# Experts' weights loaded with neighbouring rows in a partition, and transposes that take every 8th and every 2nd column

## The chip, the cores and the metric

The kernel runs on one core of a Trainium2 chip. The metric is the time of the program on the device, in microseconds (us), as the median of several runs. The engines are named as in the profile: PE is TensorE's matmuls and PEld its weight loads, DVE is VectorE, ACT is ScalarE, POOL is GpSimd and SP is SyncE, which here only issues DMAs. An engine's name with a q (SPq) is its sequencer.

## What is computed

One step of a one-layer encoder for 640 tokens (512 of a new stream, 8 x 16 of running ones): projections, a short convolution, differential attention, a gated merge, a layer norm, and then a mixture of experts. Only the last part is touched. Each token goes to 2 of 32 experts:

```
def expert_step(acc, ws):
    wgu, wd, g = ws
    a, b = jnp.split(x @ wgu, 2, axis=-1)
    return acc + g[:, None] * ((jax.nn.silu(a) * b) @ wd), None
```

`wgu` is w_gate_up of one expert, 1024 x 512 in float32 (2 MB), and `wd` is w_down, 256 x 1024 (1 MB). Everything is float32. A product of two float32 matrices is made of three matmuls on parts: an operand is split into a rounded part (hi, type fp32r) and the rest (lo), and hi x hi, hi x lo and lo x hi are added up in PSUM.

## The kernel before

`project_and_attend` does the projections and attention (up to about 820 us), `route` the output product, the norm and the choice of experts, `run_experts` the experts, `combine` the weighted sum and the last norm. The order on each engine is written out by hand, with semaphores between the engines.

`run_experts` goes through 32 blocks of up to 128 token rows, one for each expert (a spare stretch for experts with more tokens isn't entered when none has more). All that a block j needs is double buffered by its parity, except the split weights of gate and up, which exist once. Its steps, by engine:

- SP (`body` in the sync block) loads w_gate_up into `up_raw` (tiles first_up and second_up, by parity) when DVE has split the one before in that buffer (wait on `up_lo_done`), then w_down into `down_raw` (first_down, second_down) when `down_lo_done` allows. A partition holds rows p, p + 128, p + 256, ... (`(k p) n -> p k n`): 8 separate rows of 2 KB of w_gate_up, 2 of 4 KB of w_down. The loads of experts 0 to 2 are issued in `route` (`load_expert`, L1004 and L1007), the others at L1353 and L1355.
- POOL gathers the block's token rows from h_rows in HBM into `rows` (L1368, an indirect DMA of up to 128 rows of 4 KB; a place without a token moves no row) and scatters finished rows to y_choice (L1375). Its order is gather j + 2, scatter j - 1, gather j + 3, scatter j, ...; a scatter waits until ACT and DVE have both copied their half of the result.
- PE (`body`): `turn_rows` of block j + 1 (8 transposes of 128 x 128, L1403, four into each of two PSUM banks), `gate_up` of j (24 matmuls with 512 columns, L1413 to L1415), `down` of j - 1 (12, L1435 to L1437), `turn_act` of j (2 transposes, L1423).
- ACT: copies the turned rows as xT_hi (L1474), splits w_down (L1469, 2 casts) and w_gate_up (L1462, 4 casts), Silu (L1491), copies the left half of the result (L1480), aT_hi (L1498).
- DVE: xT_lo (L1521, 2), the rest part of w_down (L1534, 2) and of w_gate_up (L1515, 4), act_rows (L1540), the right half of the result (L1527), aT_lo (L1546).

In a transpose the data are PE's stationary operand (they are read by the weight load) and the identity is streamed. The contraction of gate and up runs over 1024 features, 128 at a time: the transpose k gives the 128 features that must stand on the same partitions as the weights' rows of part k.

Of the kernel before, what the change touches and what calls it, by code (L numbers as in the profile page):

```python
# [32 lines left out]
P = 128  # L33
D = 1024
KT = D // P
# [893 lines left out]
def route(nc, d, keep):  # L929

    with ExitStack() as ctx:
# [5 lines left out]
        ident = const[:, C_ID:C_ID + P]  # L937

        up, down = keep["up_raw"][0], keep["down_raw"][0]
# [44 lines left out]
        @block.sync  # L984
        def _(sp):
            for k in range(2, KT):
                sp.dma_start(w_raw[k], d["w_out"][0, P * k:P * (k + 1), :]).then_inc(w_loaded[k], 16)
            for k in range(2, 4):
                sp.dma_start(x_rows[:, k - 2], d["x_prompt"][0, P * (k - 2):P * (k - 1), :]).then_inc(x_loaded[k - 2], 16)
            sp.dma_start(column[:], d["const"][:, C_COLUMN:C_END]).then_inc(small_in, 16)  # L990
            sp.dma_start(ln_g, d["ln1_g"].to_broadcast((P, D))).then_inc(small_in, 16)
            sp.dma_start(ln_b, d["ln1_b"].to_broadcast((P, D))).then_inc(small_in, 16)
            sp.dma_start(b_router[:, 0:4], d["b_group"].to_broadcast((P, 4))).then_inc(small_in, 16)
            sp.dma_start(b_router[:, 4:36], d["b_router"].to_broadcast((P, 32))).then_inc(small_in, 16)
            sp.dma_start(w_router[:, :, 0:4], d["w_group"][0].rearrange("(k p) n -> p k n", p=P)).then_inc(small_in, 16)
            sp.dma_start(w_router[:, :, 4:36], d["w_router"][0].rearrange("(k p) n -> p k n", p=P)).then_inc(small_in, 16)

            def load_expert(e, par):

                if e == 0:  # L1000
                    sp.wait_ge(split_lo, KT)
                if e > 1:
                    sp.wait_ge(keep["up_lo_done"], 4 * (e - 1))
                sp.dma_start(keep["up_raw"][par][:], d["w_gate_up"][0, e].rearrange("(k p) n -> p k n", p=P)).then_inc(keep["up_in"][par], 16)  # L1004
                if e > 1:
                    sp.wait_ge(keep["down_lo_done"], 2 * (e - 1))
                sp.dma_start(keep["down_raw"][par][:], d["w_down"][0, e].rearrange("(k p) n -> p k n", p=P)).then_inc(keep["down_in"][par], 16)  # L1007

            load_expert(0, 0)
            for b in range(2, TB):  # L1010
                src = d["x_prompt"][0, P * b:P * (b + 1), :] if b < QB else d["x_sample"].rearrange("s q d -> (s q) d")

                sp.wait_ge(taken, b - 1)
                sp.dma_start(x_rows[:, b % 2], src).then_inc(x_loaded[b % 2], 16)
            for b in range(TB):
                sp.wait_ge(h_ready, b + 1)
                sp.dma_start(d["h_rows"][P * b:P * (b + 1), :], h[:, b, :]).then_inc(h_stored[b % 2], 16)

            sp.wait_ge(out_done, TB)
            load_expert(1, 1)  # L1020

            sp.dma_start(keep["ln2_g"], d["ln2_g"].to_broadcast((P, D))).then_inc(keep["ln2_in"], 16)
            sp.dma_start(keep["ln2_b"], d["ln2_b"].to_broadcast((P, D))).then_inc(keep["ln2_in"], 16)
            load_expert(2, 0)
            sp.wait_ge(h_stored[0], 48)
            sp.wait_ge(h_stored[1], 32)
# [261 lines left out]
def run_experts(nc, d, keep):  # L1288


    with ExitStack() as ctx:
# [4 lines left out]
        ident = const[:, C_ID:C_ID + P]  # L1296

        up_raw, down_raw, (up_hi, up_lo), (down_hi, down_lo) = keep["up_raw"], keep["down_raw"], keep["up_parts"], keep["down_parts"]
        rows, y_rows = keep["rows"], keep["y_rows"]
        xT_hi, xT_lo = sb("xT_hi", [P, 2, KT, P], F32R), sb("xT_lo", [P, 2, KT, P], F32R)  # L1300
        silu, act_rows = sb("silu", [P, DE]), sb("act_rows", [P, DE])
# [3 lines left out]
        bank_x = [pb("bank_x0"), pb("bank_x1")]  # L1305
        bank_a = pb("bank_a")
# [3 lines left out]
        up_in, down_in, up_hi_done, up_lo_done, down_hi_done, down_lo_done = (  # L1310
            keep[n] for n in ("up_in", "down_in", "up_hi_done", "up_lo_done", "down_hi_done", "down_lo_done"))
# [26 lines left out]
        @block.sync  # L1338
        def _(sp):
            def body(j, n, par, first, last):  # L1340
                if not isinstance(j, int) and keep["spare"]:
                    e = sp.value_load(eid[0:1, bass.ds(j - EXPERTS, 1)], min_val=0, max_val=EXPERTS - 1)
                elif keep["spare"]:
                    e = sp.value_load(eid[0:1, j - EXPERTS:j - EXPERTS + 1], min_val=0, max_val=EXPERTS - 1)
                else:
                    e = j if isinstance(j, int) else sp.snap(j)
                up = d["w_gate_up"][0, bass.ds(e, 1)].rearrange("a (k p) n -> p (a k) n", p=P)
                down = d["w_down"][0, bass.ds(e, 1)].rearrange("a (k p) n -> p (a k) n", p=P)
                if isinstance(j, int) and j < 3:
                    return  # L1350

                wait(sp, up_lo_done, 4 * j - 4)
                sp.dma_start(up_raw[par][:], up).then_inc(up_in[par], 16)  # L1353
                wait(sp, down_lo_done, 2 * j - 2)
                sp.dma_start(down_raw[par][:], down).then_inc(down_in[par], 16)  # L1355

            def stretch(j0, j1):
                keep["spare"] = j0 > 0
                run(sp, body, j0, j1)

            all_blocks(sp, stretch)
# [32 lines left out]
        @block.tensor  # L1394
        def _(pe):
            def turn_rows(j, n, par):
                pe.wait_ge(rows_in[par], 16 * (n + 1))
                for half in range(2):

                    wait(pe, x_lo_done, 2 * j - 1 + half)  # L1400
                    for k in range(4):
                        kk = 4 * half + k
                        last = pe.transpose(bank_x[half][:, P * k:P * (k + 1)], rows[:, par, P * kk:P * (kk + 1)], ident)  # L1403
                    last.then_inc(x_turned, 1)

            def gate_up(j, par):
                pe.wait_ge(x_lo_done, 2 * j + 2)

                wait(pe, act_done, j - 1)
                for k in range(KT):  # L1410
                    if k % 2 == 0:
                        pe.wait_ge(up_lo_done, 4 * j + k // 2 + 1)
                    pe.matmul(bank_g[par][:], xT_hi[:, par, k, :], up_hi[:, k, :], start=(k == 0), stop=False)  # L1413
                    pe.matmul(bank_g[par][:], xT_hi[:, par, k, :], up_lo[:, k, :], start=False, stop=False)  # L1414
                    last = pe.matmul(bank_g[par][:], xT_lo[:, par, k, :], up_hi[:, k, :], start=False, stop=(k == KT - 1))  # L1415
                    if k % 2 == 1:
                        last.then_inc(up_used, 1)

            def turn_act(j):
                pe.wait_ge(act_done, j + 1)  # L1420
                wait(pe, a_lo_done, j)
                for k in range(2):
                    last = pe.transpose(bank_a[:, P * k:P * (k + 1)], act_rows[:, P * k:P * (k + 1)], ident)  # L1423
                last.then_inc(a_turned, 1)

            def down(j, par):
                pe.wait_ge(a_lo_done, j + 1)

                wait(pe, y_left, j)
                wait(pe, y_right, j)  # L1430
                for k in range(2):
                    pe.wait_ge(down_lo_done, 2 * j + k + 1)
                    for strip in range(2):
                        cols = slice(512 * strip, 512 * (strip + 1))
                        pe.matmul(bank_d[strip][:], aT_hi[:, k, :], down_hi[:, par, k, cols], start=(k == 0), stop=False)  # L1435
                        pe.matmul(bank_d[strip][:], aT_hi[:, k, :], down_lo[:, par, k, cols], start=False, stop=False)
                        last = pe.matmul(bank_d[strip][:], aT_lo[:, k, :], down_hi[:, par, k, cols], start=False, stop=(k == 1))  # L1437
                    last.then_inc(down_used, 1)

            def body(j, n, par, first, last):  # L1440
                if not last:
                    turn_rows(j + 1, n + 1 if par else n, 1 - par)
                gate_up(j, par)
                if not first:
                    down(j - 1, 1 - par)
                turn_act(j)

            def stretch(j0, j1):
                turn_rows(j0, j0 // 2, 0)
                run(pe, body, j0, j1)  # L1450
                down(j1 - 1, (j1 - 1) % 2)

            all_blocks(pe, stretch)
# [272 lines left out]
```

## Time and profile before

| | |
|---|---|
| median of 3 runs | 1324.09 us (1317.96 to 1324.95) |
| span of the profiled execution | 1320.7 us |
| PE busy | 1195.9 us, 91% |
| PE weight loads busy | 1062.5 us, 80% |
| DVE busy | 758.8 us, 57% |
| ACT busy | 588.1 us, 45% |
| DMA moved | 210.37 MB in 194986 packets, mean 159 GB/s |

Every row of the trace is from one execution, so sums of rows are made against its span of 1320.7 us. A share of busy time is a mean over stages with different limits; the experts' stage is about the last quarter. The time of a DMA "to landing" runs from its issue by the engine to its last byte. A packet is one contiguous piece moved by one of the 16 DMA engines; a DMA from or to 128 partitions is spread over all 16. q1 is the queue of DMAs that SP issues, q0 of those that POOL issues.

### The profile page before, as it was taken

The numbers are of one execution on the slowest core, as the hardware profiler recorded it, in microseconds if no ns is written. First come the engines' busy times: TensorE is split into PE (matmuls) and PEld (weight loads), VectorE is DVE, ScalarE is ACT, GpSimd is POOL, SyncE is SP. The second block draws the span as 40 slices with busy tenths as digits, with TensorE's granted clock in tenths as the row PEclk, the third lists the DMA queues.
The fourth block names the chain that finished last, engine by engine and source line by source line (L and its number), as shares of the span: only waits on it lengthen the run. The fifth ranks groups of instructions, "written<-read, shape, count | busy, mean of one in ns | idle before, by whom it ended". The sixth has DMA issues, their size and how long they took to land. (4 is left out here: it accounts for less than half of the span.)

```text
span 1320.7 us, 20288 instructions
## 1 busy us (share of the span) xinstructions
PE 1195.9 (91%) x7032; PEld 1062.5 (80%) x7032; DVE 758.8 (57%) x1358; ACT 588.1 (45%) x998; POOL 110.7 (8%) x96
## 2 busy tenths in 40 slices
PE   6999999999999999999989998982788999889965
PEld 5999999899998999989879897872677777677742
DVE  4325264352643526445265555448688998888936
ACT  3232333333344242442456433221677777677722
POOL 2000000000000000000000000004112122222212
PEclk9999999999999999999989998985799999999988
DMA  6522415234152331514313244625499999999814
GB/s 154 163 85 71 126 56 151 68 89 119 43 151 67 102 107 52 153 55 114 115 56 87 78 128 181 197 75 195 152 313 330 321 332 340 337 339 320 300 49 200
DMA packets 194986, 210.37 MB, mean 159 GB/s; under 512 B 14322, under 2 KB 141810, under 8 KB 194948
## 3 DMA queue, kind: packets, MB, share of 16 engines
q1 hardware_dynamic: 171680, 188.07, 44.1%
q0 software_dynamic: 9664, 11.11, 2.5%
q10 hardware_dynamic: 13604, 10.69, 2.4%
q8 instruction: 22, 0.36, 0.1%
q14 instruction: 16, 0.13, 0.0%
HBM read 200.19 MB, written 32.71 MB: 176 GB/s over the span
## 5 line engine op out<-in xcount | busy, mean ns | idle before, releaser
L318 PE MATMUL bank_u<-x_hi,w_hi 128*128 128x320 f32 (+1 forms) x1024 | 323.9, 316 | 0.4 <-ACT hist_T L512 0.4
L319 PE MATMUL bank_u<-x_lo,w_hi 128*128 128x320 f32 (+1 forms) x1024 | 319.5, 312 | 0.0
L320 PE MATMUL bank_u<-x_hi,w_lo 128*128 128x320 f32 (+1 forms) x1024 | 318.6, 311 | 0.0
L318 PEld LDWEIGHTS bank_u<-x_hi,w_hi 128*128 128x128 f32 x1024 | 193.4, 189 | 8.6 <-issue 6.5
L320 PEld LDWEIGHTS bank_u<-x_hi,w_lo 128*128 128x128 f32 x1024 | 193.4, 189 | 0.0
L319 PEld LDWEIGHTS bank_u<-x_lo,w_hi 128*128 128x128 f32 x1024 | 193.3, 189 | 0.0
L691 DVE TENSOR_TENSOR w_lo<-w_raw,w_hi 128x1024 fp32r<-128x1024 f32 x80 | 97.8, 1223 | 153.8 <-ACT w_hi L501 153.2
L561 ACT ACTIVATE prob<-bank_s,neg_max 128x512 f32<-128x512 f32 (+4 forms) x80 | 45.7, 571 | 148.6 <-DVE neg_max L759 148.4
L1413 PE MATMUL bank_g<-w_hi_space,xT_hi 128*128 128x512 f32 x256 | 105.2, 411 | 0.0
L1414 PE MATMUL bank_g<-w_lo_space,xT_hi 128*128 128x512 f32 x256 | 101.7, 397 | 0.0
L1415 PE MATMUL bank_g<-w_hi_space,xT_lo 128*128 128x512 f32 x256 | 101.6, 397 | 0.0
L501 ACT CAST w_hi<-w_raw 128x1024 fp32r<-128x1024 f32 x80 | 83.5, 1044 | 37.2 <-issue 14.5
L1515 DVE TENSOR_TENSOR w_lo_space<-second_up,w_hi_space 128x1024 fp32r<-128x1024 f32 x64 | 75.7, 1220 | 3.4 <-ACT w_hi_space L1462 2.8
L1113 POOL MEMSET rows<- 128x2048 f32 x1 | 1.8, 1804 | 869.5 <-PE rbank L1040 869.5
L1403 PE MATMUL bank_x<-const_sb,rows 128*128 128x128 f32 x256 | 37.3, 293 | 37.7 <-DMA rows<-h_rows,token 37.0
L1515 DVE TENSOR_TENSOR w_lo_space<-first_up,w_hi_space 128x1024 fp32r<-128x1024 f32 x60 | 71.0, 1221 | 0.5 <-ACT w_hi_space L1462 0.2
L1462 ACT CAST w_hi_space<-second_up 128x1024 fp32r<-128x1024 f32 x64 | 64.4, 1057 | 3.4 <-PE bank_g L1415 3.3
L1403 PEld LDWEIGHTS bank_x<-const_sb,rows 128*128 128x128 f32 x256 | 29.7, 148 | 43.4 <-issue 33.4
L1521 DVE TENSOR_TENSOR xT_lo<-bank_x,xT_hi 128x512 fp32r<-128x512 f32 x64 | 41.6, 687 | 34.0 <-ACT xT_hi L1474 21.6
L1462 ACT CAST w_hi_space<-first_up 128x1024 fp32r<-128x1024 f32 x60 | 60.4, 1054 | 1.5 <-PE bank_g L1415 1.4
L1474 ACT CAST xT_hi<-bank_x 128x512 fp32r<-128x512 f32 x64 | 35.1, 594 | 53.8 <-PE bank_x L1403 53.6
L1415 PEld LDWEIGHTS bank_g<-w_hi_space,xT_lo 128*128 128x128 f32 x256 | 49.2, 192 | 11.0
(318 smaller groups left out, 2324.1 us busy)
## 6 DMA issues: line engine op xcount, KB each, us to landing
w_raw<-in_w_in SPq DMA_DIRECT2D x64, 512.0 KB, 4.1
first_up<-in_w_gate_up SPq DMA_DIRECT2D x16, 2048.0 KB, 10.6
second_up<-in_w_gate_up SPq DMA_DIRECT2D x16, 2048.0 KB, 10.6
first_down<-in_w_down SPq DMA_DIRECT2D x16, 1024.0 KB
second_down<-in_w_down SPq DMA_DIRECT2D x16, 1024.0 KB
k_cache<-in_cache_k SPq DMA_DIRECT2D x16, 512.0 KB
v_cache<-in_cache_v SPq DMA_DIRECT2D x16, 512.0 KB
w_raw<-in_w_branch SPq DMA_DIRECT2D x16, 512.0 KB, 4.3
```

The lines of the kernel that those rows point to most:

```text
L318: pe.matmul(out, w_hi[:, u % 2, k, :], x_hi[:, k, cols], start=(k == 0), stop=False)
L319: pe.matmul(out, w_hi[:, u % 2, k, :], x_lo[:, k, cols], start=False, stop=False)
L320: last = pe.matmul(out, w_lo[:, u % 2, k, :], x_hi[:, k, cols], start=False, stop=(k == KT - 1))
L501: act.copy(w_hi[:, u % 2], w_raw[:, u % 2]).then_inc(s["split_hi"], 1)
L561: act.activation(prob[:, m, 0:w], bank_s[m][:, 0:w], ACT.Exp, bias=neg_max[:, m:m + 1], scale=SCALE, accum_out=row_sum[:, m:m + 1]).then_i ...
L691: v.tensor_tensor(w_lo[:, u % 2], w_raw[:, u % 2], w_hi[:, u % 2].bitcast(F32), ALU.subtract).then_inc(s["split_lo"], 1)
L1403: last = pe.transpose(bank_x[half][:, P * k:P * (k + 1)], rows[:, par, P * kk:P * (kk + 1)], ident)
L1413: pe.matmul(bank_g[par][:], xT_hi[:, par, k, :], up_hi[:, k, :], start=(k == 0), stop=False)
L1414: pe.matmul(bank_g[par][:], xT_hi[:, par, k, :], up_lo[:, k, :], start=False, stop=False)
L1415: last = pe.matmul(bank_g[par][:], xT_lo[:, par, k, :], up_hi[:, k, :], start=False, stop=(k == KT - 1))
L1462: act.copy(up_hi[:, 2 * x:2 * x + 2, :], up_raw[par][:, 2 * x:2 * x + 2, :]).then_inc(up_hi_done, 1)
L1515: v.tensor_tensor(up_lo[:, s, :], up_raw[par][:, s, :], up_hi[:, s, :].bitcast(F32), ALU.subtract).then_inc(up_lo_done, 1)
```

## The change

Which rows of an expert's weights stand in a partition: 8 neighbouring rows of w_gate_up and 2 neighbouring rows of w_down, where before it was every 128th row. Part k of the contraction is then made of features k, k + 8, k + 16, ... (for w_down k, k + 2, ...), so the transposes take every 8th column of the token rows and every 2nd column of act_rows. Sizes, counts, waits and the order on every engine stay.

```diff
@@ route: load_expert
-                sp.dma_start(keep["up_raw"][par][:], d["w_gate_up"][0, e].rearrange("(k p) n -> p k n", p=P)).then_inc(keep["up_in"][par], 16)
+                sp.dma_start(keep["up_raw"][par][:], d["w_gate_up"][0, e].rearrange("(p k) n -> p k n", p=P)).then_inc(keep["up_in"][par], 16)
...
-                sp.dma_start(keep["down_raw"][par][:], d["w_down"][0, e].rearrange("(k p) n -> p k n", p=P)).then_inc(keep["down_in"][par], 16)
+                sp.dma_start(keep["down_raw"][par][:], d["w_down"][0, e].rearrange("(p k) n -> p k n", p=P)).then_inc(keep["down_in"][par], 16)
@@ run_experts: sync
-                up = d["w_gate_up"][0, bass.ds(e, 1)].rearrange("a (k p) n -> p (a k) n", p=P)
-                down = d["w_down"][0, bass.ds(e, 1)].rearrange("a (k p) n -> p (a k) n", p=P)
+                up = d["w_gate_up"][0, bass.ds(e, 1)].rearrange("a (p k) n -> p (a k) n", p=P)
+                down = d["w_down"][0, bass.ds(e, 1)].rearrange("a (p k) n -> p (a k) n", p=P)
@@ run_experts: turn_rows
-                        last = pe.transpose(bank_x[half][:, P * k:P * (k + 1)], rows[:, par, P * kk:P * (kk + 1)], ident)
+                        last = pe.transpose(bank_x[half][:, P * k:P * (k + 1)], rows[:, par, :].rearrange("s (p k) -> s k p", k=KT)[:, kk, :], ident)
@@ run_experts: turn_act
-                    last = pe.transpose(bank_a[:, P * k:P * (k + 1)], act_rows[:, P * k:P * (k + 1)], ident)
+                    last = pe.transpose(bank_a[:, P * k:P * (k + 1)], act_rows[:].rearrange("s (p k) -> s k p", k=2)[:, k, :], ident)
```

## Rows read from the trace of the kernel before

**Rows 1.** The page's part 2: busy tenths in 40 equal slices of the span.
```profile
PE   6999999999999999999989998982788999889965
...
DVE  4325264352643526445265555448688998888936
...
DMA  6522415234152331514313244625499999999814
```

**Rows 2.** 30 us: busy PE, PEld, DVE, ACT, POOL (instructions), clock, DMA share, GB/s.
```profile
1040.00:1070.00 30.00, 28.46 (x138) 23.31 (x138) 28.16 (x34) 23.89 (x33) 6.67 (x6) 1.00 0.92 321
```

**Rows 3.** Timeline of POOL: start us, us, engine, line, operation [idle before <-releaser].
```profile
956.32 2.03 POOL L1368 DMA_INDIRECT rows<-h_rows,token  x1 [0.30 <-issue]
...
1042.38 1.01 POOL L1368 DMA_INDIRECT rows<-h_rows,token  x1 [0.30 <-issue]
...
1052.71 1.02 POOL L1368 DMA_INDIRECT rows<-h_rows,token  x1 [0.30 <-issue]
...
1063.00 1.58 POOL L1368 DMA_INDIRECT rows<-h_rows,token  x1 [0.31 <-issue]
...
1242.69 1.58 POOL L1368 DMA_INDIRECT rows<-h_rows,token  x1 [0.30 <-issue]
```

**Rows 4.** Timeline of SP's queue, one load of w_gate_up.
```profile
1050.09 0.37 SPq L1353 DMA_DIRECT2D second_up<-in_w_gate_up  x1
```

**Rows 5.** Timeline of DVE, one round.
```profile
1051.54 1.29 DVE L1521 TENSOR_TENSOR xT_lo<-bank_x,xT_hi 128x512 fp32r<-128x512 f32 x2 [0.68 <-ACT xT_hi L1474]
...
1060.12 0.69 DVE L1527 COPY y_rows<-bank_d 128x512 f32<-128x512 f32 x1
...
1061.06 1.28 DVE L1521 TENSOR_TENSOR xT_lo<-bank_x,xT_hi 128x512 fp32r<-128x512 f32 x2
```

**Rows 6.** Timeline of PE, the row transposes of three rounds.
```profile
1050.24 1.09 PE L1403 MATMUL bank_x<-const_sb,rows 128*128 128x128 f32 x8 [0.77 <-DMA rows<-h_rows,token]
...
1070.02 1.09 PE L1403 MATMUL bank_x<-const_sb,rows 128*128 128x128 f32 x8 [0.80 <-DMA rows<-h_rows,token]
1070.87 0.48 PE L1413 MATMUL bank_g<-w_hi_space,xT_hi 128*128 128x512 f32 x1
...
1079.37 1.03 PE L1403 MATMUL bank_x<-const_sb,rows 128*128 128x128 f32 x8
```

**Rows 7.** Waits, 950 to 1240 us: waiter <- releaser, us in total, times, longest.
```profile
PE bank_x L1403 <- DMA rows<-h_rows,token: 27.3, 18, 3.2
ACT xT_hi L1474 <- PE bank_x L1403: 27.1, 18, 3.2
DVE xT_lo L1521 <- ACT xT_hi L1474: 13.3, 12, 2.0
```

**Rows 8.** Landing: second_up from 950; gathered rows from 950; gathered rows, 920 to 950.
```profile
DMA to landing us min/median/max: 9.3/10.8/13.3
...
DMA to landing us min/median/max: 6.5/7.8/9.8
...
DMA to landing us min/median/max: 4.0/4.2/4.4
```

**Rows 9.** Timeline of ACT: first casts of second_up.
```profile
1063.28 2.95 ACT L1462 CAST w_hi_space<-second_up 128x1024 fp32r<-128x1024 f32 x3
```

**Rows 10.** DMA queues (packets, MB, share of 16 engines) in 950:1240, 300:700, 1283:1300.
```profile
q1 hardware_dynamic: 35982, 86.50, 84.4%
q0 software_dynamic: 7776, 9.33, 8.9%
...
q1 hardware_dynamic: 58490, 30.48, 27.4%
...
q1 hardware_dynamic: 1440, 5.24, 79.6%
```

**Rows 11.** PE's weight loads by group: x count | busy us, mean ns; first 950 to 1240.
```profile
L1403 PEld LDWEIGHTS bank_x<-const_sb,rows 128*128 128x128 f32 x222 | 24.2, 141 | 32.2 <-issue 32.1
...
L1074 PEld LDWEIGHTS bank_c<-both,ones 128*128 128x128 f32 x2 | 0.6, 338 | 0.0
```

## The prediction

> **What bounds the kernel now.** The page first: slices of the span [rows 1]. The reader is to see two regimes. Up to slice 27 TensorE is at 9 and DMA low; from slice 29 to 37, the expert stage, DMA stands at 9 and DVE at 8 or 9. The change touches only loads and transposes of that stage, so everything else is left alone. In a stretch of 30 us of it [rows 2] PE has 28.46 us of work, DVE 28.16, DMA a share of 0.92: nobody is alone at the limit, and shares don't tell who sets the pace. So I followed one round (an expert) through the timelines.
>
> The pace: 28 gathers of token rows are issued on POOL from 956.32 to 1242.69 [rows 3], 27 rounds in 286.4 us, 10.61 us each. Some rounds are shorter: DVE starts xT_lo at 1051.54 and at 1061.06, 9.52 us [rows 5]; PE starts its row transposes at 1070.02 and 1079.37, 9.35 us [rows 6], and the rows that end these rounds name no wait. These are the floors: PE 9.35, DVE about 9.5. What is above them, 1.1 us a round or 27 x 1.1 = 30 us in the stage, is a wait. The waits [rows 7] name it: PE before the row transposes (L1403) waits for the gathered rows, 27.3 us in 18 times; ACT's xT_hi behind it waits 27.1 us in 18; DVE's xT_lo behind that 13.3. Weights come in time in the middle of the stage: an up load issued at 1050.09 lands 10.8 us later in the median [rows 8], and its first cast by ACT is at 1063.28 [rows 9], 2.4 us after.
>
> The gather's loop spans two rounds: issue 1042.38 [rows 3], row transposes 1050.24 [rows 6] (7.86 later), xT_lo 1051.54 [rows 5] (1.30), DVE's work until y_rows ends at 1060.12 + 0.69 = 1060.81 [rows 5] (9.27), then POOL's scatter and, behind it, the next gather of this chain at 1063.00 [rows 3] (2.19). The sum is 20.62, or 10.31 a round, and what varies in it is the first term, the landing G: 6.5/7.8/9.8 us in the stage, against 4.0/4.2/4.4 before the loads run [rows 8]. So 3.6 us of G are time in which the gather's pieces stand behind the weight loads in the 16 DMA engines.
>
> **The change, part by part.**
>
> Bytes: none added or removed. Each load stays one DMA of 2 MB or 1 MB from SP, at its place in the queue; nothing is moved past anything, no wait is added.
>
> Packets. A partition of w_gate_up now reads 8 rows of 2 KB that lie 256 KB apart; after it reads 16 KB in one run. For w_down 2 runs of 4 KB become one of 8 KB. In the stage q1 has 35982 packets of 86.50 MB at 84.4% [rows 10]: 0.844 x 290 us x 16 / 35982 = 109 ns each at 2404 B; about 80 a round and engine (64 of 2 KB, 16 of 4 KB). Two mixes give the fixed part: 0.274 x 400 x 16 / 58490 = 30.0 ns at 521 B, and 0.796 x 17 x 16 / 1440 = 150 ns at 3641 B [rows 10]. The slope is 120 / 3120 = 38.6 ns a KB, the rest 10 ns a packet. 80 packets become 16: 64 x 10 ns = 0.64 us less a round and engine, out of 80 x 109 ns = 8.7 us. The line gives 103 ns at 2404 B where 109 was measured, so 6 ns more a packet are stalls; if they go by packet, another 64 x 6 = 0.4 us. Hence 0.6 to 1.0 us less DMA work in each round. The trace has no load of 16 KB runs; from below the saving is 0 (long runs stall more, or the chip cuts them), from above 1.0.
>
> What it is worth. The loads themselves are not waited for, so it counts only through G. I let G fall by the saving and a little more, since the end of the up load is what stands ahead of the gather's pieces: 7.8 to about 6.5. Bounds: 4.2 (unloaded), a fall of 3.6; and above, 9.8, the worst now. With 6.5 the loop is 20.62 + (6.5 - 7.86) = 19.3, 9.65 a round, just over DVE's floor; next late is DVE. Rounds that vary (G by 1.5 either way) and are cut off at 9.5 from below come to about 9.9. Gain: 27 x (10.61 - 9.9) = 19 us. If G fell to 4.2 all would stand at 9.5: 30 us.
>
> Transposes. 8 row transposes (L1403) and 2 of act_rows (L1423) a round keep number and size, but their weight loads read 128 columns at a step of 32 B and 8 B in a partition. No row of this trace has such a step. The nearest are the same loads packed, 141 ns [rows 11], and the ends are 0 more and the slowest weight load of that size anywhere, 338 ns [rows 11], 198 ns more. I take 0, as the row nearest in form, engine and place has it: transposes follow each other every 0.11 us (8 in 0.85 us, from 1070.02 to the next matmul at 1070.87 [rows 6]), the packed load is 0.14 and runs beside the matmul before. It is not free if it grows: nothing covers it. PE's floor takes all of it, and it is in the loop as well, between landing and xT_lo. At the upper end PE's floor is 9.35 + 10 x 0.198 = 11.3 us: 27 x 0.7 = 19 us slower.
>
> Here a rule of the Trainium skill speaks against the change. Its page "SBUF — State Buffer" (under "Door 1: The DMA port swizzle") and "Advanced Engine Details and Errata" ("SBUF Cachelines") say that SBUF is read in lines of 16 bytes and that an access pattern needs at least two hits in a line for full rate. A step of 32 B has one hit a line, one of 8 B has two, so by the rule only the 8 row transposes would suffer; it gives no figure. No row here shows it; it is the second rival below.
>
> ACT's and DVE's instructions read the same banks in the same shapes: 0.
>
> **The sum.** Profiled span 1320.7 us, the median of the runs 1324.1, 3.4 above; 1320.7 - 19 = 1302, and 1324.1 - 19 = 1305. I say 1306, a little less gain because the first rounds and the last few have other limits.
>
> **The rivals.**
>
> First, slower: the gather waits longer, because what it waits behind are packets of 16 KB. On POOL's queue are 7776 packets in 27 rounds [rows 10], 18 a round and engine (9 for the scatter, 9 for the gather). If engines take turns between the queues packet by packet, each piece now waits for about 0.1 us of weights, after the change for 10 ns + 16384 x 0.0386 = 0.64 us, and 0.33 for down. The 18 pieces would then end only as the loads' last packets end. A round's work on an engine is 8.7 - 0.64 = 8.1 us of loads and 0.089 x 290 / 27 = 0.96 us of pieces, 9.0 us from the up issue on, and the gather is issued 2.6 us after that (1050.09 [rows 4] to 1052.71 [rows 3]): G is at least 6.4 on an engine that works without a hole, and on one that lags it may reach the worst of today or more. With G at 9.8, 2 us more, a round takes 1.0 more: 27 us slower, 1351. It decides from G above 7.8. For it: 18 pieces against 16 load packets, and G is the last of 16 engines. Against: the pieces already stand behind most of the up load, in whatever size, and all of the queue gets shorter. The page "DMA: Bandwidth & Descriptors" of the Trainium skill ("Queues, rings and completion order") says that an engine does take turns between its rings, by packet, with several descriptors in one; what the turns cost at this size no row shows.
>
> Second, the step of 32 B halves the rate of the row transposes' weight loads. Then each of the 8, of 0.11 us now, costs 0.11 more: PE's floor is 9.35 + 0.87 = 10.2, the loop 20.2 / 2 = 10.1. With the gather's gain kept, a round is 10.2 to 10.3: 27 x 0.35 = 9 us faster, 1315. Without that gain (G stays 7.8) the loop is 10.6 + 0.43: 12 us slower, 1336; at the bound of 338 ns 1343. Nothing in the trace speaks against it but that the packed loads have the time of the matmuls they hide beside.
>
> Third, nothing to measure: the 16 KB runs are cut into short packets, or G is set by POOL's own writing of its pieces and not by the loads. 1324, within 5 us. Against: 4.2 unloaded and 7.8 loaded.
>
> **How the numbers follow.** Forecast 0.40 (1306, its own range 1293 to 1316); gather later 0.20 (1351); slower transposes 0.25 (1315 to 1343, a third of it on the fast side); nothing 0.15 (1324). What a measurement of this kernel can tell from no change is about 0.5%, 6.6 us. Faster: 0.38 + 0.08 = 0.46; within: 0.02 + 0.05 + 0.13 = 0.20; slower: 0.20 + 0.12 + 0.02 = 0.34. The range leaves out about 0.05 below 1292 (30 us are all there is to win) and the worse half of the first rival above 1346.
>
> **What would show it.** Packets: q1 about 7200 to 8500 in the stage instead of 35982, its share near 78%. The gather's landing: median near 6.5 (forecast), near 7.8 (third), above 9 (first). PE's wait for gathered rows from 27 us to under 10. L1403's weight load at 141 ns (forecast) or near 250 (second), and the 8 transposes in 0.85 or 1.7 us. Rounds from 10.6 to 9.9. I would be wrong if the landing did not follow the loads' work, or if rounds with early rows took more than 9.5.

## The result: 1349 us, slower by 2.1%

Median of four runs of the changed kernel 1349.05 us (1344.23 to 1359.67); of the kernel before, beside it on the same chip, 1323.76. The ratio is 1.0208, interval 1.0157 to 1.0259 (the two medians alone are 25 us, 1.9%, apart). So it is slower, clear of the noise, by somewhere between 1.6% and 2.6%. The forecast was 1306 with a range from 1292 to 1346; the sign is wrong. The first rival, 1351 with a landing of 9.8 us, is what happened, though its number is in part luck: it priced the later landing alone, and a second cost, told below, makes up for a landing that grew less than it said. The profiled execution was the slowest of the four (span 1357.8 us, run 1359.67), so its rows show some 11 us more than the median does.

The page's slices of the changed kernel, to be held against [rows 1], and after them the clock slices of the kernel before:
```profile
PE   6999999999999999999899989926888898888965
...
DVE  4325253453526435264536556486778887778946
...
PEclk9999999999999999999899999956899998889988
DMA  6523315242151522415123337253878877878714
```
```profile
PEclk9999999999999999999989998985799999999988
```
In most slices of the expert stage PE, DVE and the DMA have lost a tenth or more against before, where DMA stood at 9 from the 30th to the 37th slice. Less of everything per time: a wait has grown. The granted clock has three 8s there (34th to 36th slice) where before it had only 9s.

Its queues and its landings from 950 to 1240 us (queue: packets, MB, share of 16 engines; load: median us from issue to landing), against [rows 10] and [rows 8]:
```profile
q1 hardware_dynamic: 7015, 76.46, 72.7%
q0 software_dynamic: 6879, 8.74, 8.3%
...
second_up<-in_w_gate_up SPq DMA_DIRECT2D x12, 2048.0 KB, 10.1
...
rows<-h_rows,token POOLq DMA_INDIRECT x24, 9.6
```
And the gathered rows from 950 to 1250 us, minimum, median and maximum:
```profile
DMA to landing us min/median/max: 6.9/9.5/13.0
```
The change does what it says: 7015 packets where 35982 were. The up load itself lands earlier (10.1 us against 10.8). The gathered rows land later, 9.5 against 7.8. The window ends before the changed kernel's stage does: over all of its 28 gathers the median is 8.9 (6.1 to 13.0), still against 7.8.

The waits of the same stretch (waiter <- releaser: us, times, longest), against [rows 7], and then three row transposes:
```profile
ACT xT_hi L1474 <- PE bank_x L1403: 45.4, 23, 7.1
...
DVE xT_lo L1521 <- ACT xT_hi L1474: 43.5, 21, 6.9
...
PE bank_x L1403 <- DMA rows<-h_rows,token: 41.5, 16, 6.6
```
```profile
1060.47 1.16 PE L1403 MATMUL bank_x<-const_sb,rows 128*128 128x128 f32 x8
1061.38 0.48 PE L1413 MATMUL bank_g<-w_hi_space,xT_hi 128*128 128x512 f32 x1
...
1133.58 1.97 PE L1403 MATMUL bank_x<-const_sb,rows 128*128 128x128 f32 x8 [6.59 <-DMA rows<-h_rows,token]
...
1144.95 1.06 PE L1403 MATMUL bank_x<-const_sb,rows 128*128 128x128 f32 x8
```
PE's wait for rows went from 27.3 us to 41.5, and one of them is 6.6 us long. The whole stage, by POOL's gathers as in [rows 3]:
```profile
956.90 2.03 POOL L1368 DMA_INDIRECT rows<-h_rows,token  x1 [0.30 <-issue]
...
1278.18 1.68 POOL L1368 DMA_INDIRECT rows<-h_rows,token  x1 [0.30 <-issue]
```
These are 27 rounds in 321.3 us, 11.90 each, against 10.61: 35 of the 37 us by which the two spans differ.

### The profile page after: what moved, and what is told of

The parts are those of the page before. It is cut to its first block and busy times, and to the rows that moved or that the text cites. A ratio compares the mean times of both kernels' runs of the same rounds, so it can differ in the third digit from the quotient of the medians.

```text
span 1357.8 us, 20288 instructions
## 1 busy us (share of the span) xinstructions
PE 1214.6 (89%) x7032; PEld 1080.0 (80%) x7032; DVE 763.4 (56%) x1358; ACT 591.8 (44%) x998; POOL 112.5 (8%) x96
## 5 line engine op out<-in xcount | busy, mean ns | idle before, releaser
L1413 PE MATMUL bank_g<-w_hi_space,xT_hi 128*128 128x512 f32 x256 | 110.1, 430 | 0.0
L1414 PE MATMUL bank_g<-w_lo_space,xT_hi 128*128 128x512 f32 x256 | 106.4, 416 | 0.0
L1415 PE MATMUL bank_g<-w_hi_space,xT_lo 128*128 128x512 f32 x256 | 105.7, 413 | 0.0
L1403 PE MATMUL bank_x<-const_sb,rows 128*128 128x128 f32 x256 | 43.1, 321 | 55.9 <-DMA rows<-h_rows,token 55.2
L1403 PEld LDWEIGHTS bank_x<-const_sb,rows 128*128 128x128 f32 x256 | 35.8, 201 | 60.4 <-issue 50.5
L1413 PEld LDWEIGHTS bank_g<-w_hi_space,xT_hi 128*128 128x128 f32 x256 | 53.3, 208 | 10.6
```

## The experiments

Every kernel was timed beside the kernel before (medians 1323.8 to 1326.6). Landing is that of the gathered rows from 950 to 1250 us, minimum/median/maximum, in one execution of each kernel; where the trace names none it is left out.

| kernel | median us | ratio (interval) | landing us |
|---|---|---|---|
| the change | 1349.05 | 1.0208 (1.0157 to 1.0259) | 6.9/9.5/13.0 |
| dma_only | 1351.92 | 1.0186 (1.0149 to 1.0223) | 5.7/8.9/12.3 |
| turn_only | 1327.78 | 1.0005 (0.9988 to 1.0022) | 6.4/8.0/9.9 |
| up_only | 1346.31 | 1.0142 (1.0115 to 1.0170) | 5.5/8.2/12.5 |
| down_only | 1336.76 | 1.0088 (1.0059 to 1.0116) | 6.7/8.3/9.7 |
| packets_4k | 1338.56 | 1.0078 (1.0050 to 1.0105) | 6.0/8.3/11.2 |
| packets_8k | 1341.24 | 1.0109 (1.0088 to 1.0129) | 5.8/8.3/11.6 |
| cut_runs | 1329.72 | 1.0031 (1.0009 to 1.0053) | 6.3/8.1/10.2 |
| late_down | 1352.68 | 1.0192 (1.0151 to 1.0232) | 6.8/9.9/11.8 |
| late_down_before | 1322.01 | 0.9971 (0.9948 to 0.9993) | 7.1/7.8/9.2 |
| small_down_before | 1313.28 | 0.9917 (0.9894 to 0.9941) | 6.5/7.5/8.6 |
| small_down_after | 1307.21 | 0.9879 (0.9828 to 0.9930) | 5.7/6.9/7.9 |
| early_before | 1307.28 | 0.9849 (0.9830 to 0.9867) | 6.6/7.8/9.3 |
| early_after | 1296.21 | 0.9762 (0.9743 to 0.9781) | not shown |
| early_cut_runs | 1298.95 | 0.9784 (0.9744 to 0.9824) | not shown |

### Loads or transposes

**dma_only**: the changed kernel with the transposes of before. Features and weights don't meet in this one and the next, so neither computes the layer; sizes and counts of the work stay. Where a cut of code shows one of several like edits, "..." stands for the others.
```diff
-  ...rows[:, par, :].rearrange("s (p k) -> s k p", k=KT)[:, kk, :], ident)
+  ...rows[:, par, P * kk:P * (kk + 1)], ident)
...
```


> The loads of the change alone (16 KB and 8 KB runs); the transposes are those of before, so features and weights don't match and the output leaves the reference: that part of the computation is changed. Landing theory (long packets make the last engine's share of the gathered rows late): the whole loss stays, 1345 to 1353, gather landing median about 9 us, PE's wait for gathered rows 40 us or more. Transpose theory (slower weight loads at a step): within 3 us of before, 1321 to 1327.

**turn_only**: the loads of before with the changed transposes (edit against the change).
```diff
-  d["w_gate_up"][0, bass.ds(e, 1)].rearrange("a (p k) n -> p (a k) n", p=P)
+  d["w_gate_up"][0, bass.ds(e, 1)].rearrange("a (k p) n -> p (a k) n", p=P)
...
```


> The strided transposes alone, with the loads of before; the output leaves the reference for the same reason. Transpose theory: 1340 to 1350 and the 8 row transposes take longer than the 1.09 us of before. Landing theory: no difference, 1320 to 1327, although the weight load of a transpose goes from 141 to about 195 ns, since it runs beside the matmul before it and the 8 transposes still take 1.05 to 1.2 us.

PE's wait for rows in dma_only, then in turn_only with its two groups of weight loads (950 to 1240 us: times | busy us, mean ns | idle before):
```profile
PE bank_x L1403 <- DMA rows<-h_rows,token: 39.5, 16, 4.3
```
```profile
PE bank_x L1403 <- DMA rows<-h_rows,token: 26.3, 21, 2.6
...
L1403 PEld LDWEIGHTS bank_x<-const_sb,rows 128*128 128x128 f32 x216 | 26.9, 195 | 30.7 <-issue 30.7
...
L1423 PEld LDWEIGHTS bank_a<-const_sb,act_rows 128*128 128x128 f32 x54 | 10.4, 197 | 2.4 <-DVE act_rows L1540 0.3
```
The loads alone give the whole loss (1.0186 against 1.0208, intervals that overlap), the transposes none. The strided weight loads do take longer, 195 ns against 141 in [rows 11], and it costs nothing (1.0005).

**up_only** and **down_only**: only one of the two weights laid anew, with its own transposes. The edit of up_only against the change:
```diff
-  down = d["w_down"][0, bass.ds(e, 1)].rearrange("a (p k) n -> p (a k) n", p=P)
+  down = d["w_down"][0, bass.ds(e, 1)].rearrange("a (k p) n -> p (a k) n", p=P)
...
```


> w_gate_up in 16 KB runs with its transposes, w_down as before. Landing theory with the long up packets as the cause: most of the loss, 1338 to 1350, landing 8.5 us or more. If instead the down load, which arrives at the engines just when the gather's pieces do, is the cause: 1315 to 1327.

> w_down in 8 KB runs with its transposes, w_gate_up as before. Landing theory with the up packets as the cause: 1320 to 1330, landing 7.5 to 8.2 us. If the down load is the cause: 1335 or more, landing 8.5 us or more.

Both lose, 1.4% and 0.9%; the sum, 2.3%, is about the 2.1% of the change. So neither load alone is the cause, which both expectations had as a choice. The landings fell short of the 8.5 us expected: 8.2 in the median of up_only with 12.5 at worst, 8.3 in down_only, whose traced execution was the fastest of its six (1328.0 where their median is 1336.8) and shows little of its loss.

### Length of a packet

**packets_4k**, **packets_8k**: 2 or 4 neighbouring rows of w_gate_up in a run, w_down as before, with transposes at a step of 2 or 4. The edit of packets_4k against the kernel before:
```diff
-  up = ...rearrange("a (k p) n -> p (a k) n", p=P)
+  up = ...rearrange("a (c p b) n -> p (a c) b n", p=P, b=2)
...
```


> w_gate_up with 2 neighbouring rows in a run (4 runs of 4 KB a partition), w_down as before (4 KB), transposes at a step of 2 to match. Landing theory, by packet length: about as before, 1312 to 1328, landing 7 to 8.3 us; if 10 ns a packet counts at all it shows here as a gain. Transpose theory: the loss grows with the step, so 1324 to 1330 here.

> w_gate_up with 4 neighbouring rows in a run (2 runs of 8 KB a partition), w_down as before, transposes at a step of 4. Landing theory: between before and the change, 1325 to 1340, landing 8 to 9 us. Transpose theory: 1340 or more, since a step of 16 B already has one hit in a line.

The loss rises with the run: 0.8% at 4 KB, 1.1% at 8 KB, 1.4% at 16 KB (up_only), the latest landing with it, 11.2, 11.6, 12.5 us. The intervals of neighbours overlap; only the ends differ clearly. More than half of the loss is there at 4 KB already, the length that w_down's packets always had: 1338.6 us lies outside both expectations of packets_4k, and 1341.2 is just above the landing theory's range for packets_8k.

**cut_runs**: everything of the change, the same addresses in the same places, but each load in two DMAs of every second row, so that no packet is longer than 2 KB (w_down 4 KB). The waits on these loads count both DMAs.
```diff
-  sp.dma_start(up_raw[par][:], up).then_inc(up_in[par], 16)
+  for x in range(2):
+      sp.dma_start(up_raw[par][:, x::2, :], up[:, x::2, :]).then_inc(up_in[par], 16)
...
```


> The changed kernel with each load cut into two DMAs of every second row, so the placing in the partitions and the addresses in HBM are those of the change, but packets are 2 KB and 4 KB as before. If the length of a packet makes the gather late: back to about the kernel before, 1320 to 1332, landing median 7.5 to 8.3. If it is where the engines read in HBM (neighbouring rows of one partition, engines 64 KB apart): it stays at 1340 or more.

Its queue and its wait in the same stretch:
```profile
q1 hardware_dynamic: 36239, 84.84, 82.9%
...
PE bank_x L1407 <- DMA rows<-h_rows,token: 28.0, 16, 3.2
```
With short packets again 1.0031: nearly all of the loss is gone though rows, partitions and transposes are those of the change. So where the rows lie isn't enough to cost the time. What the edit took away is the length of the packets, but it also made two DMAs of each load, and this run doesn't separate the two. That the loss rises with the run while each load is one DMA (packets_4k, packets_8k, up_only) speaks for the length.

### What stands ahead of the gather

**late_down** (and **late_down_before** on the kernel before): SP issues w_down's load only when the rows of this block have landed.
```diff
+  sp.wait_ge(rows_in[par], 16 * (n + 1))
   sp.dma_start(down_raw[par][:], down).then_inc(down_in[par], 16)
```


> The changed kernel, in which SP issues the w_down load of a block only after that block's gathered rows have landed, so that no w_down packets stand beside the gather's pieces. If the pieces are late because they queue with the 8 KB packets of w_down on engines that lag: landing median under 7.5 and 1300 to 1325. If they wait for the 16 KB packets of w_gate_up: landing stays near 9, 1340 or more.

> The same wait on the kernel before. If w_down's packets stand before the pieces there too: landing median under 7.5, 1305 to 1320. If the down load is then too late for ACT's split or the engines idle too long: 1330 or more. If w_down's packets play no part: 1320 to 1328.

In late_down landing stayed late (9.9) and the time too: the expectation of a landing under 7.5 fell. The wait doesn't take w_down out of the gather's way, it moves it to just before the next up load (in its trace w_down's is issued at 1046.60, the up load at 1047.21, the gather at 1047.61), and then both stand ahead of the next gather's pieces. The run can't tell the two loads apart. On the kernel before the same wait left the landing at 7.8 and the time 0.3% shorter, inside the range expected if w_down's packets play no part there.

**small_down_before**, **small_down_after**: from expert 3 on, w_down's load brings 16 of its 1024 columns and the rest of the buffer keeps old weights. This leaves transfers of the computation out.
```diff
-  sp.dma_start(down_raw[par][:], down).then_inc(down_in[par], 16)
+  sp.dma_start(down_raw[par][:, :, 0:16], down[:, :, 0:16]).then_inc(down_in[par], 16)
```


> The kernel before, w_down's load for experts 3 to 31 cut to 16 of its 1024 columns (the rest of its part of the computation uses stale weights). A third of the load traffic is gone. Both theories: the gather's wait shrinks, landing median 6.5 to 7.5, 1300 to 1318.

> The same on the changed kernel. If the last engine's pieces are late because the whole w_down load (8 packets of 0.31 us) comes to stand ahead of them there: landing median within 0.5 us of the one before it, 1300 to 1320. If they wait for an engine's 16 KB packets of w_gate_up whatever w_down does: the landing stays 1 us or more above, and the time 10 us or more.

PE's wait and the landing, first of small_down_before, then of small_down_after:
```profile
PE bank_x L1403 <- DMA rows<-h_rows,token: 19.7, 22, 1.5
...
DMA to landing us min/median/max: 6.5/7.5/8.6
```
```profile
PE bank_x L1403 <- DMA rows<-h_rows,token: 10.4, 14, 1.9
...
DMA to landing us min/median/max: 5.7/6.9/7.9
```
With w_down's bytes gone, the up loads in runs of 16 KB no longer hurt: rows land 0.6 us earlier than with short ones, and the time, 1307.2, is not above the 1313.3 of small_down_before (two runs and three; the intervals of the ratios overlap). So a long packet isn't bad by itself. It is bad where more is queued ahead of the gather's pieces; whether that is w_down's packets as such or only fuller engines (DMA share 0.93 in the kernel before, 0.71 and 0.68 here, 950 to 1240 us) this pair doesn't tell. No other row of the table has a median landing that long packets made earlier, as the forecast had it.

### The gather one place earlier

**early_before**, **early_after**: POOL issues a gather ahead of the scatter behind which it stood.
```diff
+  gather(j0 + 2)
   for j in range(j0, j1):
-      if j + 2 < j1:
-          gather(j + 2)
+      if j + 3 < j1:
+          gather(j + 3)
       if j > j0:
           scatter(j - 1)
```


> The kernel before, but POOL issues the gather of block j + 3 ahead of the scatter of block j - 1 instead of behind it, so the rows are asked for nearly a round earlier. Both theories on the kernel before say its rounds above the floors are waits for gathered rows: PE's wait for them goes from 27 us to under 8, a round from 10.6 to 9.6 or 9.9, 1298 to 1308. If the rounds are long for another reason (weights, DMA rate): 1318 or more.

> The changed kernel with the same early gather. Landing theory: the loss of the change goes with the wait, 1296 to 1310, within 5 us of the early gather on the kernel before, although landings stay at 9 us or more in the median. Transpose theory: 20 us or more above the early gather on the kernel before.

In the kernel before a gather is issued just after the row transposes of the block ahead of it and has one round to land. Here it is issued just after those of two blocks ahead, which free its buffer, and has two rounds. What is then left of waits, first in early_before, which names none for rows, and then in early_after, where the last line is its windows view (window, length, busy PE, PEld, DVE, ACT, POOL with instructions, clock, DMA share, GB/s):
```profile
DVE w_lo_space L1516 <- ACT w_hi_space L1463: 14.9, 18, 1.8
ACT w_hi_space L1463 <- DMA second_up<-in_w_gate_up: 11.1, 9, 1.8
PE bank_a L1424 <- DVE act_rows L1541: 10.8, 16, 1.5
ACT w_hi_space L1463 <- DMA first_up<-in_w_gate_up: 10.4, 9, 2.2
```
```profile
PE bank_x L1404 <- DMA rows<-h_rows,token: 5.4, 13, 0.7
...
950.00:1240.00 290.00, 284.08 (x1373) 236.67 (x1372) 280.65 (x328) 235.82 (x326) 71.73 (x57) 1.00 0.92 342
```
In early_after PE is busy for 284 of 290 us at full clock and DVE for 281; nothing waits for weights. It is the fastest of all, 1296.21 us, 2.4% under the kernel before and 53 us under the change. In early_before ACT waits 21.5 us for the up weights, DVE behind it, and PE at the end of that row for act_rows. The same layout costs 25 us with the gather late and gives 11 us (1307.28 to 1296.21) with it early: what the layout does to the time is decided by whether a landing is on the path.

**early_cut_runs**: both edits together, to see whether those 11 us come from the packets' fixed time.


> The early gather on the changed kernel with short packets. If the 11 us between the early gather on the changed kernel (1296) and on the kernel before (1307) are the fixed time of a packet (64 x 10 ns a round), it is at 1304 to 1310 with ACT waiting for weights again, 15 us or more; if they come from where the engines read, 1294 to 1300.

1298.95 us with 2 KB packets: only some 3 of the 11 us go with the length of a packet, and its interval and that of early_after overlap. The other 8 go with the placing of the rows or with the cut into two DMAs, which these runs don't separate. The time is where the expectation had it for "where the engines read", but ACT again waits for weights, 10.6 us in all, half of early_before's.

## Why the prediction was wrong

**Right.** The bound: PE waiting for the gathered rows, behind a loop of two rounds, above floors of 9.35 and 9.5 us. Taking that wait away gave 30 us in early_after (1326.62 to 1296.21 beside its own runs of before), where the floors had promised 30. That agreement is in part luck: in the traces it is 23 us (1320.7 to 1297.5), since a round there is 9.77 us and not 9.5, and 27 x (10.61 - 9.77) = 23. On the layout of before it gave 19: what is late next there is ACT on its weights, not DVE as I wrote. Also the price of a long packet: the line of 10 ns and 38.6 ns a KB gave 0.64 us for 16 KB, and the trace of the change has a median of 611 ns.

**The saving was mis-sized.** I had 0.6 to 1.0 us of DMA work less in each round and engine. The two loads of a round are 3.146 MB; q1's share and bytes give 0.844 x 290 / (86.50 / 3.146) = 8.90 us a round before and 0.727 x 290 / (76.46 / 3.146) = 8.68 after, 0.22 less. The step that failed is "if they go by packet, another 64 x 6 = 0.4 us": the stalls did not get fewer with the packets. By medians the fixed part did come, 64 x 84 + 16 x 159 = 7.92 us before and 8 x 611 + 8 x 309 = 7.36 after, 0.56 less. But packets of 16 KB took 733 ns in the mean against their median of 611, those of 2 KB 97 against 84, and what a round's means lie above its medians grew from about 1.0 to 1.3 us. That took back more than half.

**The step that decided.** "I let G fall by the saving and a little more, since the end of the up load is what stands ahead of the gather's pieces." That step takes the landing to follow the engines' mean work. It follows the last of the 16. Each engine adds one to the semaphore when its share is there; from these updates, in the mean of 28 gathers, us after issue, in the order in which the engines finish (which engine is which the trace doesn't tell):

| | 1st engine | 8th | 12th | 15th | last |
|---|---|---|---|---|---|
| before | 5.57 | 6.32 | 7.05 | 7.56 | 7.92 |
| the change | 4.76 | 5.54 | 6.69 | 7.95 | 9.43 |

For the first 12 engines the forecast was right: the pieces come 0.4 to 0.8 us earlier. On the last they come 1.5 us later, and the block waits for that one. In cut_runs it is 7.99 again, in small_down_after 6.78 (small_down_before 7.47). With one of the loads lengthened it is 8.26 in down_only, 8.47 in packets_4k, 8.38 in packets_8k and 8.48 in up_only: in the mean the last engine is no later with 16 KB than with 4 KB, and only both loads together, the change and dma_only (9.05), bring it over 9. The rival's text had the term ("on one that lags it may reach the worst of today or more"); I gave it 0.20 because all of the queue gets shorter, which is an argument on the mean.

**Where 35 us in the trace come from.** The last engine's 1.5 us later, over a loop of two rounds, is 0.75 a round, 27 x 0.75 = 20 us by this estimate. The other 15 I had not priced, nor had the first rival, whose 27 us are landing alone; they fit the granted clock. Windows of the change (columns as in [rows 2]): the stage, a round with a long wait, and the round behind it, cut in two; then the same stage before.
```profile
950.00:1290.00 340.00, 293.38 (x1330) 243.57 (x1329) 277.26 (x318) 233.28 (x318) 67.61 (x57) 0.93 0.80 292
...
1117.45:1133.58 16.13, 9.54 (x49) 7.80 (x47) 10.57 (x13) 8.72 (x13) 5.09 (x4) 0.92 0.88 325
...
1133.58:1137.89 4.31, 4.31 (x15) 3.75 (x15) 2.13 (x3) 2.90 (x4) 0.00 (x0) 0.50 0.39 152
1137.89:1144.95 7.06, 7.06 (x34) 5.87 (x33) 6.67 (x7) 4.66 (x6) 0.00 (x0) 1.00 0.42 152
```
```profile
950.00:1255.00 305.00, 276.61 (x1331) 227.26 (x1330) 273.00 (x318) 230.34 (x319) 65.90 (x57) 0.99 0.92 326
```
After 6.59 us idle for rows (the transposes at 1133.58 above) PE works 4.3 us at a granted clock of 0.50, its level of 1.2 GHz, then at 1.00 again. A matmul of 512 columns follows the one before in 0.43 us there and in 0.23 after. The round takes 11.37 us with no wait in it, against 9.35: this long wait costs 2 us more in the next round. Of 28 rounds, taken between row transposes, 13 have a mean clock under 0.97; before it were 2, in cut_runs 3, in early_after none. The 13 hold eleven stretches at 0.50 between 950 and 1290 us; the sum of their windows:
```profile
sum 44.38, PE 39.63 PEld 33.22 DVE 25.91 ACT 32.37 POOL 9.20; mean PE 3.60 PEld 3.02 DVE 2.36 ACT 2.94 POOL 0.84
```
PE works in 39.6 of these 44.4 us, at half its rate, so about 19.8 us are lost. The kernel before has two such stretches, 6.8 us, which is 3.4 lost. The difference, 16 us, fits the 15; that the two causes add up without overlap is not shown.

**The second rival fell.** It had weight loads near 250 ns and transposes in 1.7 us. They took 199 ns in the change and the 8 transposes 0.91 us (1060.47 to 1061.38 above) against 0.85 in [rows 6]: longer, but still beside the matmul before. My value of 0 was right, its reason (the packed duration of 141) was not. The prediction's "nothing covers it" fell too: the matmul before did. The **third** fell with 7015 packets and the 2%.

## What stays open

Which rule makes the last engine late. Before, a piece stood among packets of 0.1 us; with 16 KB each load packet is 0.6 us. If a piece goes after a bounded number of load packets, not bytes, an engine that lags when w_down and the next up load are queued delays its pieces by whole long packets. cut_runs and small_down_after fit this; that 16 KB in the up load alone bring the last engine no later than 4 KB do (8.48 and 8.47 us) speaks against it as the whole story. No run shows an engine's choice between its queues, so this is argued.

The Trainium skill, page "DMA: Bandwidth & Descriptors", section "Queues, rings and completion order", says an engine takes turns between its rings by packet. By that rule longer packets on one ring give the other ring's pieces less of the engine, which agrees with 9.43 against 7.92 us on the last engine; it doesn't tell why the 12 first engines deliver earlier. What the page calls a packet holds several descriptors, and the trace does not show how its own records are grouped into them, so the agreement is one of direction only.

The same page's "Rules for kernel authors" would have many small transfers coalesced into a large one. Here each load was one DMA of 2 MB or 1 MB already and only its packets grew; the trace has 8.68 against 8.90 us a round for it, and the landing of another queue's pieces 1.5 us later.

And why early_after beats early_before by 11 us when packets explain about 3. With the gather early, more of the forecast's saving in DMA work is there. The queue of the loads in early_before, early_after and early_cut_runs, 950 to 1240 us:
```profile
q1 hardware_dynamic: 37248, 89.59, 86.6%
...
q1 hardware_dynamic: 8260, 89.72, 82.5%
...
q1 hardware_dynamic: 38207, 89.69, 85.7%
```
Worked out as above these are 8.82, 8.39 and 8.72 us a round. So early_after saves 0.4 us of the 0.6 to 1.0 forecast, 0.3 of them with the long packets, and yet the kernel without them, at 8.72, is within 3 us of the fastest.

## What to carry to other kernels

Before making the packets of a large load longer, look for small DMAs of another queue that start behind it and are waited for: they land with the last of the 16 engines, and that one may come later while most of the others come earlier. If one is on the path, first issue it earlier (here a gather one place ahead of a scatter, 1.5% on the kernel before); the same layout of weights then turned from 2.1% slower into the fastest kernel. And price a repeated wait of PE at more than its length, as the round behind it may run at the lower clock.

## What the runs showed of the hardware

- Time of a packet of these loads by length, median and mean ns: 2 KB 84 and 97, 4 KB 159 and 169, 8 KB 309 and 348, 16 KB 611 and 733. Nearly proportional; a packet's fixed part is about 10 ns (2 x 84 - 159 = 9 by the medians).
- A weight load of 128 columns of f32 took 139 to 154 ns packed in the mean (141 in the kernel before) and 194 to 212 at a step of 2, 4 or 8 elements (of the row transposes 211 at 2, 212 at 4, 194 to 199 at 8); the largest step is no slower than the smaller. packets_4k has a step of 2 in its row transposes and none in the other (950 to 1240 us), and the change has 8 and 2:
```profile
L1403 PEld LDWEIGHTS bank_x<-const_sb,rows 128*128 128x128 f32 x208 | 30.0, 211 | 37.1 <-issue 36.9
...
L1423 PEld LDWEIGHTS bank_a<-const_sb,act_rows 128*128 128x128 f32 x52 | 7.2, 139 | 3.4
```
```profile
L1403 PEld LDWEIGHTS bank_x<-const_sb,rows 128*128 128x128 f32 x192 | 25.9, 199 | 44.7 <-issue 44.7
...
L1423 PEld LDWEIGHTS bank_a<-const_sb,act_rows 128*128 128x128 f32 x48 | 9.0, 198 | 2.4 <-DVE act_rows L1540 0.7
```
  By the rule of the Trainium skill that the prediction cites (page "SBUF — State Buffer", at least two hits in a line of 16 bytes for full rate), the step of 8 B, which has two, should have stayed at the packed time. It went from 139 to 198 and 211 ns, so here the trace does not agree.
- With the long packets the first 12 of the 16 engines to finish delivered another queue's pieces earlier and the last one later (4.76 to 9.43 us over the 16, against 5.57 to 7.92).
- After 6.6 us without work PE ran its next 4.3 us at a granted clock of 0.50 (1.2 GHz). Over the expert stage the changed kernel had eleven stretches at 0.50, of 3.4 or 6.8 us, the kernel before two, early_after none.
